# A norm's sum of squares kept in two halves and multiplied by ones in two float32 matmuls instead of one

## What is computed

```python
def rmsnorm(x, g):
    x32 = x.astype(jnp.float32)
    y = x32 * lax.rsqrt(jnp.mean(x32 * x32, axis=-1, keepdims=True) + EPS)
    return (y * g.astype(jnp.float32)).astype(x.dtype)
...
        h = h + merged @ w_out
        hn = rmsnorm(h, norm_ffn_g)
        u = causal_dwconv(hn @ w_up, ffn_conv_w, ffn_conv_b)
        gate, val = jnp.split(u, 2, axis=-1)
        h = h + (jax.nn.silu(gate) * val) @ w_down
```

## Time and profile before

| | us |
|---|---|
| median of 3 runs | 2228.18 (2225.63 to 2228.34) |
| the profiled execution's own time | 2226.45 |
| its span in the profile | 2224.7 |
| PE busy | 2145.7 (96%) |
| DVE, ACT, POOL busy | 1312.7, 1158.4, 283.3 |
| mean granted TensorE clock | 0.985 of full |

### The profile page before, as it was taken

One profiled execution on the slowest core, in us unless ns is written; L12 is line 12 of the kernel. 1 busy time (PEld: TensorE's weight loads), 2 busy tenths in 40 slices (PEclk: granted clock), 3 DMA queues, 4 the chain that ended last, 5 costly groups with the idle time before them and its releaser, 6 DMA issues.

```text
span 2224.7 us, 46503 instructions
## 1 busy us (share of the span) xinstructions
PE 2145.7 (96%) x17596; PEld 2104.9 (95%) x17596; DVE 1312.7 (59%) x1641; ACT 1158.4 (52%) x1544; POOL 283.3 (13%) x325
## 2 busy tenths in 40 slices
PE   5999999999999999999999999999999979999996
PEld 5999999999999999999999999999998969899996
DVE  5655664544557666666765545655665465755644
ACT  5444545555546555555554444644554445656542
POOL 2000000010110111111111100001010123111112
PEclk8999999999999999999999999999999989999998
DMA  4454545555555555555545555445444434444453
GB/s 150 172 183 174 189 163 198 194 187 202 189 189 192 186 188 189 187 183 181 187 186 208 193 218 212 146 178 190 171 169 170 171 131 147 157 151 152 155 183 113
DMA packets 54927, 393.83 MB, mean 177 GB/s; under 512 B 6097, under 2 KB 6225, under 8 KB 7522
## 3 DMA queue, kind: packets, MB, share of 16 engines
q1 hardware_dynamic: 54432, 392.19, 49.2%
q10 hardware_dynamic: 450, 1.02, 0.1%
HBM read 391.09 MB, written 2.10 MB: 177 GB/s over the span
## 4 chain that ended last, share of the span: by engine, by line
PE 80%; issue 13%; POOL 3%; DVE 2%; ACT 2%; DMA 0%; POOLq 0%; DVEq 0%; ACTq 0%
PE acc L554 23%; PE acc L555 23%; PE acc L556 23%; PE tok L596 2%; PE tok L598 2%; PE tok L597 2%; POOL n_lo L1927 1%; POOL sumsq_g L1918 1%; PE att L614 1%; POOL x L1940 0%; POOL probs L2080 0%; DVE rstd L1345 0%; POOL probs L2077 0%; PE att L788 0%; PE att L864 0%
## 5 line engine op out<-in xcount | busy, mean ns | idle before, releaser
L1337 DVE TENSOR_TENSOR w_lo<-raw,w_hi 128x1024 fp32r<-128x1024 f32 x740 | 907.0, 1239 | 728.2 <-ACT w_hi L921 726.1
L921 ACT ACTIVATE w_hi<-raw 128x1024 fp32r<-128x1024 f32 x740 | 770.0, 1056 | 594.7 <-PE acc L556 363.5
L554 PE MATMUL acc<-n_hi,w_hi 128*128 128x256 f32 x3488 | 986.7, 283 | 26.8 <-POOL n_lo L1927 19.4
L555 PE MATMUL acc<-n_lo,w_hi 128*128 128x256 f32 x3488 | 979.6, 281 | 0.0
L556 PE MATMUL acc<-n_hi,w_lo 128*128 128x256 f32 x3488 | 979.4, 281 | 0.0
L554 PEld LDWEIGHTS acc<-n_hi,w_hi 128*128 128x128 f32 x3488 | 668.7, 192 | 30.1 <-issue 20.2
L555 PEld LDWEIGHTS acc<-n_lo,w_hi 128*128 128x128 f32 x3488 | 662.0, 190 | 0.5
L556 PEld LDWEIGHTS acc<-n_hi,w_lo 128*128 128x128 f32 x3488 | 660.8, 189 | 0.0
L555 PE MATMUL acc<-f_lo,w_hi 128*128 128x256 f32 x688 | 193.5, 281 | 0.0
L556 PE MATMUL acc<-f_hi,w_lo 128*128 128x256 f32 x688 | 193.5, 281 | 0.0
L554 PE MATMUL acc<-f_hi,w_hi 128*128 128x256 f32 x688 | 193.5, 281 | 0.0
(11 more groups left out here) (313 smaller groups left out, 2950.8 us busy)
## 6 DMA issues: line engine op xcount, KB each, us to landing
raw<-stream_in SPq DMA_DIRECT2D x370, 1024.0 KB, 4.8
x<-x_in SPq DMA_DIRECT2D x4, 512.0 KB, 7.4
out<-x SPq DMA_DIRECT2D x4, 512.0 KB, 2.6
v_bias<-v_bias_in ACTq DMA_DIRECT2D x1, 512.0 KB, 8.9
par<-params_in ACTq DMA_DIRECT2D x1, 287.0 KB, 5.5
pos_i<-positions_in ACTq DMA_DIRECT2D x1, 128.0 KB, 6.8
gk<-gk_in ACTq DMA_DIRECT2D x1, 68.0 KB
```

The source lines that it names most:

```text
L554: nc.tensor.matmul(out, w_hi[:, s, wc], hi[:, k, :], start=first, stop=False)
L555: nc.tensor.matmul(out, w_hi[:, s, wc], lo[:, k, :], start=False, stop=False)
L921: nc.scalar.activation(w_hi[:, s, :], raw[:, s, :], ACT.Copy).then_inc(hi_ready, 1)
L1337: nc.vector.tensor_tensor(w_lo[:, s, :], raw[:, s, :], w_hi[:, s, :].bitcast(fp32), ALU.subtract).then_inc(lo_ready, 1)
```

## The change

The squares of odd tiles (m = 1) are added to a second sum, `sumsq_odd`, which lies where `f_val` of the up stage will be and is set to zero by one memset more. The new `norm_sum_ffn` multiplies `ones` by both sums, in two float32 matmuls that accumulate in the same bank. The waits on `sq_added` stay as they were, and the other norms keep one sum.

```diff
--- before.py
+++ after.py
@@ -211,11 +211,13 @@
         f_lo = a.place("f_lo", [P, F_TILES, T], fp32r)
         f_pre = a.place("f_pre", [P, 2, T])
         f_gate = a.place("f_gate", [P, T])
+        f_val_at = a.at
         f_val = a.place("f_val", [P, T])
         f_silu = a.place("f_silu", [P, T])
         f_act = a.place("f_act", [P, T])
 
         square_g = a.place("square_g", [P, 2, T])
+        sumsq_odd = Arena(f_val_at).place("sumsq_odd", [P, T])
         sumsq_g = a.place("sumsq_g", [P, T])
         eps_tile = a.place("eps_tile", [P, P])
 
@@ -599,6 +601,13 @@
                                                     stop=k == n_k - 1)
                     last.then_inc(unit_done, 1)
 
+            def norm_sum_ffn():
+
+                pe.wait_ge(sq_added, FREE + KT * (POOLED["ffn"] + 1))
+                nc.tensor.matmul(att[3][:, 0:T], ones[:, :], sumsq[:, :], start=True, stop=False)
+                nc.tensor.matmul(att[3][:, 0:T], ones[:, :], sumsq_odd[:, :], start=False, stop=True)\
+                    .then_inc(stat_ready, 1)
+
             def norm_sum(n):
 
                 pe.wait_ge(sq_added, FREE + KT * (POOLED[n] + 1))
@@ -689,7 +698,7 @@
                 for m in range(2):
                     feature_tile("wout", i, 2 * m, 1 - m, 0, mg_hi, mg_lo, ready=((mglo_ready, 1),))
 
-            feature_tile("wup", 0, 0, 1, 0, n_hi, n_lo, unscaled="ffn", between=lambda: norm_sum("ffn"))
+            feature_tile("wup", 0, 0, 1, 0, n_hi, n_lo, unscaled="ffn", between=norm_sum_ffn)
             feature_tile("wup", 0, 2, 0, 0, n_hi, n_lo)
 
             def up(i):
@@ -1907,13 +1916,16 @@
                 if with_gain:
                     chain.step(gp.memset(eps_tile[:, :], EPS))
                     chain.link(gp.memset(sumsq_g[:, :], 0.0))
+                if n == "ffn":
+                    chain.step(gp.memset(sumsq_odd[:, :], 0.0))
                 chain.link(gp.memset(sumsq[:, :], 0.0))
                 with pool.Fori(0, KT // 2) as i:
                     for m in range(2):
                         pool.wait_ge(sq_ready, 2 * i + (k * KT + m + 1))
 
                         pool.wait_ge(sq_added, FREE + 2 * i + (k * KT + m))
-                        ins = gp.tensor_tensor(sumsq[:, :], sumsq[:, :], square[:, m, :], ALU.add)
+                        total = sumsq_odd if n == "ffn" and m else sumsq
+                        ins = gp.tensor_tensor(total[:, :], total[:, :], square[:, m, :], ALU.add)
                         if with_gain:
                             ins = gp.tensor_tensor(sumsq_g[:, :], sumsq_g[:, :], square_g[:, m, :], ALU.add)
                         ins.then_inc(sq_added, 1)
```

## The result

| | before | after |
|---|---|---|
| median of the runs | 2228.26 us (2225.63 to 2231.58, 4 runs) | 2200.73 us (2197.76 to 2202.78, 4 runs) |
| profiled execution, its span | 2226.45 us, 2224.7 us | 2202.78 us, 2201.1 us |

The ratio is 0.9875, with an interval of 0.9857 to 0.9892: the change makes the kernel 1.2% faster. The forecast of no change, 2228.6 us, was wrong; the first rival, 2201 us, is what happened.

The account below looks back on a forecast made before the run. The prediction took PE, 100% busy in the long projection stages, as the bound. 2226.45 us + 0.43 for the added matmul + 0 for the pitch gave 2226.9, put at 2228.6 us because the median lay 1.7 higher; range 2199 to 2231 us.

Parts of the forecast that it names:

- first rival: Behind the norm, the second matmul puts 6,192 matmuls back on the short pitch: 27.6 us less, 2201 us; chance 0.33.
- Memset: On POOL ahead of its first add of squares: one more memset of 0.31 us fits in a 3.49 us wait, cost nothing.
- two sums: POOL's 16 adds still come in order, each waiting for the count raised by the one before: no time gained.
- added matmul: On PE at the norm: the second float32 matmul of 256 columns lies on the path and costs 0.43 us.
- DVE and ACT behind the norm: Their queues move by 0.43 us against some 3 us of slack and DVE catches up: cost nothing.
- The pitch after it: Spacing of the 6,192 matmuls behind the norm: taken as unchanged, 0; the other end was 27.2 us, by starts 27.6 us.
- two-in-a-row groups of attention: Attention's scores end with two 256-column matmuls; in four places after the short pitch they left the long one, so 0 was taken.
- short pitch: Faster spacing of PE's equal projection matmuls: 884 in 100 us, 113.1 ns, mean 113.3 ns from 600 to 681 us.
- long pitch: Slower spacing of the same matmuls: 851 in 100 us, mean 117.8 ns behind the norm; forecast to stay.
- group of three: Three float32 matmuls in a row at 1411 us, after the long pitch and a short stall, left the short one.
- the two rows: One 256-column matmul after the long pitch left the short one at 94.74 us but the long one at 1889.96 us.
- second rival: From 1413 to 2113 us some 2,100 projection matmuls lose their short pitch: 9.4 us more, 2238 us; chance 0.05.

Follow-up runs that it names:

- e2: The changed kernel without its second norm matmul, so the odd tiles' squares are left out of the norm: 2226.32 us, ratio 1.0011.
- e4: The kernel before with four float32 matmuls of 256 columns in a row at the norm instead of one: 2228.12 us, ratio 1.001.
- e6: The kernel before with the norm's single float32 matmul cut into two of 128 columns each: 2226.89 us, ratio 1.0.
- e13: The kernel before plus narrow fp32r matmuls behind the norm's, gated linear attention's output sums and last norm's sums, and ahead of the last projection: 2193.46 us.
- e17: The same kernel as e13, run again on one chip with the changed kernel: 2193.66 us, ratio 0.9854.
- e11: The kernel before with one fp32r matmul of 128 columns added at 332 us, between mixer and merge stage: 2215.34 us in one run.
- e7: The kernel before with a second float32 matmul 24 projection matmuls behind the norm's, between first and second up tile: 2231.49 us in one run.
- e9: The kernel before with one fp32r matmul of 128 columns behind the second up tile, at 689.6 us: 2198.9 us in one run.
- e1: The kernel before with a second float32 matmul of 256 columns behind the norm's own, result unread, one sum kept: 2200.48 us, ratio 0.9894.
- e15: e1 with the narrow fp32r matmul of e11 added at 332 us: 2213.52 us in one run.
- e3: The kernel before with three float32 matmuls of 256 columns in a row at the norm instead of one: 2226.99 us, ratio 1.0009.
- e5: The kernel before with a second float32 matmul, of 128 columns, behind the norm's own of 256: 2201.01 us in two runs, ratio 0.9881.
- e8: The kernel before with one fp32r matmul of 128 columns right behind the norm's single float32 matmul: 2200.92 us in one run.
- e10: The kernel before with a narrow fp32r matmul behind five kinds of float32 groups: those of e13 and the mixer's mLSTM heads: 2236.01 us, ratio 1.0037.
- e14: The changed kernel with the narrow fp32r matmul of e9 added at the same place: 2223.89 us in one run.
- e12: The kernel before with one fp32r matmul of 256 columns right behind the norm's single float32 matmul: 2222.22 us in one run.

## Why the prediction was wrong

**The added parts: right.** Memset nothing, two sums nothing, since each add waits for its square: the rows of POOL and e2. The added matmul 0.43 us: the rows of PE. DVE and ACT behind the norm: the first product comes 5.40 us behind the norm's first matmul (685.90 - 680.50), before it was 5.41, and nobody waits.

**The pitch after it: wrong, and this is the whole miss.** The size was right: 27.6 us forecast for the first rival, 27.50 measured (its factors as rounded there, 6,192 x 4.5 ns, give 27.9). The range of 2199 to 2231 us reached the measured time only because it was stretched to that rival, which had a chance of 0.33. What failed is the step that took the two-in-a-row groups of attention as the model for the norm's, because they were nearest in form. That group is a row of twelve float32 matmuls of 128 and 256 columns (four products with the probabilities, L864 and L865, then eight of the scores), of which the two are only the end, and e4 to e6 show how much hangs on what else a group holds: four instead of two, or twice 128 columns instead of 256 and 128, and the result is the other one. A likeness in the last two instructions decided nothing.

The evidence for the step was also picked too narrowly. "In all four places" leaves out three more places of the same trace at which the eight scores come behind the short pitch, with 24 matmuls of 512 columns and a wait of PE of 0.6 us between. One of them left the short pitch (46 matmuls in 5 us, where the long pitch leaves 45):

```profile
1970.98 0.48 PE L846 MATMUL att<-kn,qn 128*128 128x128 f32 x2 [0.62 <-DVE q_rope L1824]
...
1974.00:1979.00 5.00, 5.00 (x46) 1.00 0.54 210
```

Behind a wait, the same instructions resume on either pitch, even in the same kernel. e13 and e17 are one kernel, both come short to the group of three in a row (L724 to L726 there, with a wait of 0.34 us), and behind it e13 goes on short and e17 long:

```profile
1387.00:1392.00 5.00, 5.00 (x47) 1.00 0.60 210
```

```profile
1387.00:1392.00 5.00, 5.00 (x45) 1.00 0.62 216
```

So the group of three, which has such a wait too, told nothing about either rival. Groups without a wait are another matter. In all 20 profiles, a single float32 matmul of 256 columns that came on the short pitch left the long one, 94 times of 94. Of those that came long, 72 left short (the sum of an mLSTM head, 71 times of 71, and e11) and 18 long (the second latent sum, 17 times of 17, and e7). So the two rows are no accident of one execution.

**What the runs show in its place.**

| group behind which the stream resumes | arriving short | arriving long |
|---|---|---|
| one float32 matmul of 256 | long (before, e2, e9) | short (e11) or long (e7), see below |
| two | short (after, e1) | short (e15) |
| three; four, without a wait | long (e3); long (e4) | not tried |
| 256 and 128 of float32 | short (e5) | not tried |
| twice 128 of float32 | long (e6) | not tried |
| one of 256 float32, one narrow fp32r | short (e8, e13) | long (e10) |
| one narrow fp32r | long (e11, e14, e15) | short (e9) |
| one of 256 float32, one of 256 fp32r | long (e12) | not tried |

One, two and three would fit a simple rule by which each float32 matmul turns the pitch over; four, and twice 128, do not. So the pitch is a property of how the stream resumes, in these profiles it holds until the next group or stall, and the change is one of several ways to make it resume on the short one. *Why* it has two, no run shows. These are the starts of the records, in ns from start to start, around the norm's matmuls (a float32 matmul is two records; the first bar stands at the start of the norm's matmul, the second at that of the first projection matmul behind the group):

```
before  116 | 215  27 | 305 117 118 118 117   long
after   115 | 215 215 215  28 | 305 120 117 116 114 113 113   short
e3      three of them, then 28 | 306 120 117 119 117 118   long
```

Three short intervals in a row are 340 ns in each of the 1,176 threes from 700 to 1100 us of the changed kernel; three long ones are 353 ns on the mean, 352 to 355 ns each, in the same window of the kernel before. What in the group decides between the two is not shown: adding up the passes of a group did not forecast e4 or e6, so the rule is open.

Why a single matmul arriving long did one thing in e11 and the other in e7 is open too, but the traces show a sign that tells the two apart. The norm's matmul in e11, then the added one in e7:

```profile
697.08 0.60 PE L605 MATMUL att<-sumsq,ones 128*128 128x256 f32 x2
...
685.60 0.59 PE L693 MATMUL att<-sumsq,ones 128*128 128x256 f32 x2
```

The difference in the second column is no rounding. Of the 90 that arrive long, the 72 that leave short start their second pass 219 to 221 ns after the first, and the 18 that leave long 215 ns after it; they also start 117 to 119 ns and 120 or 121 ns behind the last matmul of the stream. So "arriving long" is at least two states. The norm's matmul of e10 has 120 and 215 ns, as those that leave the long pitch.

**The later stages** (second rival): the group of three at 1383.63 us left 54 matmuls in 6 us in this profile, the long pitch, where it left 55, the short one, and other stretches of 48 to 120 changed in both directions. That is at most some tenths of a microsecond each, below the 8 us by which two executions of the changed kernel differ there. The rival had no visible part in the result. The half-clock stretches that it names are in the traces (granted clock 0.50 from 1425.8 to 1429.2 us before, 0.51 from 1397.6 to 1401.0 us now); no run shows that they wipe out what came before.

## What to carry to other kernels

Where PE is at 100% in a long stream of equal matmuls, read the pitch from windows of equal length before and behind each foreign matmul; two counts at one clock (884 and 851 in 100 us at 1.00 in the kernel before) mean that time lies there which the busy share of PE does not show (100% in both). Then try, behind the group where it turns long, one narrow matmul into an unused bank (0.11 us here, for 27 us), and read the windows of the whole kernel again, since the same matmul in a short stretch can put it on the long pitch (e11, e14). Behind a group with a wait in it, look at several executions before you believe a pitch (47 matmuls in 5 us in e13, 45 in e17, one kernel). A neighbouring group that looks alike is no forecast for which way it goes; the run is.

## What was not expected of the hardware

- One fp32r matmul of 128 columns, 0.11 us of work, moves the time of the kernel down (e9: 2198.9 us against 2227.95) or, placed in the same spot behind the change, up (e14: 2223.89 against 2200.73 us). The stretch of 6,120 matmuls behind it takes 693.4 us in e9 and 720.6 us in e14.
- The pitch survives loop ends and the change from up to down projection: 6,192 matmuls over 700 us without a break, at 113.3 or 117.8 ns.
- Two profiled executions of the same kernel differ by 8 us in the part from 1383 us on (818.1 and 810.1 us). Some 2 us of it are the different number of matmuls on the short pitch; the rest was not traced.
